# Decay sums spread over the partitions by two transfers through DRAM instead of PE transposes, gates formed between the chunks, in a two-layer hybrid trunk (one core)

## The reference, cut to what matters

```
proj = rms_norm(h) @ w_in
y_a  = gated DeltaNet(proj) @ w_out_gdn       # 8 heads, chunks
y_b  = sparse attention(proj) @ w_out_dsa     # 8 heads
h    = h + (sigmoid(g_a) * y_a + sigmoid(g_b) * y_b) @ w_o
h    = h + swiglu(rms_norm(h))
```

```
gam   = cumsum(g)                                        # per chunk
decay = exp(gam[:, None] - gam[None, :])  for i >= j     # chunk x chunk
q_dec, k_beta_dec = q * exp(gam), k * beta * exp(gam)
```

## Time and profile before

| | us |
|---|---|
| median of 3 runs (2181.29 to 2182.16) | 2181.73 |
| the profiled execution, its own time | 2180.09 |
| its span in the profile | 2178.3 |
| PE busy (share of the span) | 2146.1 (99%) |
| DVE, ACT, POOL busy | 1140.4, 1004.5, 1054.1 (52%, 46%, 48%) |
| mean granted clock of PE, as a share of full speed | 0.998 |
| DMA engines busy | 28.4% |

### The profile page before, as it was taken

One profiled execution on the slowest core, in us unless ns is written; L12 is line 12 of the kernel. 1 busy time (PEld: TensorE's weight loads), 2 busy tenths in 40 slices (PEclk: granted clock), 3 DMA queues, 4 the chain that ended last, 5 costly groups with the idle time before them and its releaser, 6 DMA issues.

```text
span 2178.3 us, 32534 instructions
## 1 busy us (share of the span) xinstructions
PE 2146.1 (99%) x12612; PEld 1764.5 (81%) x12612; DVE 1140.4 (52%) x2267; ACT 1004.5 (46%) x2285; POOL 1054.1 (48%) x776
## 2 busy tenths in 40 slices
PE   8999999999999999999999999999999999999998
PEld 6778887888888888888877788888888888888886
DVE  7678887444533444440187788765554234444302
ACT  6656665555423333332365656745554233333222
POOL 4455554433455555554445355534434555555542
PEclk9999999999999999999999999999999999999999
DMA  4222222222233333333322222222222333333332
GB/s 156 73 63 62 65 67 64 73 77 74 78 97 97 92 97 97 97 97 97 90 80 78 64 62 62 64 69 74 77 77 79 97 97 94 98 98 96 96 98 90
DMA packets 98937, 183.07 MB, mean 84 GB/s; under 512 B 11104, under 2 KB 11360, under 8 KB 98784
## 3 DMA queue, kind: packets, MB, share of 16 engines
q1 hardware_dynamic: 98784, 180.99, 28.4%
HBM read 178.85 MB, written 2.10 MB: 83 GB/s over the span
## 4 chain that ended last, share of the span: by engine, by line
PE 90%; DVE 5%; ACT 3%; POOL 1%; issue 1%; DMA 0%; DVEq 0%; SPq 0%; POOLq 0%; ACTq 0%
PE bank L1647 87%; PE bank L1723 2%; ACT w_hi L647 1%; DVE conv_acc L1082 1%; PE bank L2032 1%; DVE bank L1079 1%; DVE ob_lo L1079 1%; DVE inv L1079 1%; POOL w_lo L557 0%; ACT conv_acc L658 0%; PE bank L1717 0%; DVE left L1294 0%; ACT p_quad L658 0%; DVE k_b L1079 0%; POOL diagonal L588 0%
## 5 line engine op out<-in xcount | busy, mean ns | idle before, releaser
L557 POOL TENSOR_TENSOR w_lo<-w_raw,w_hi 128x512 fp32r<-128x512 f32 x668 | 927.8, 1411 | 1026.5 <-ACT w_hi L647 1026.5
L1647 PE MATMUL bank<-xn_hi,w_hi 128*128 128x512 f32 x1840 | 735.8, 400 | 3.0 <-POOL w_lo L557 2.0
L1647 PE MATMUL bank<-xn_hi,w_lo 128*128 128x512 f32 x1840 | 735.2, 400 | 0.0
L1647 PE MATMUL bank<-xn_lo,w_hi 128*128 128x512 f32 x1840 | 731.7, 398 | 0.0
L647 ACT ACTIVATE w_hi<-w_raw 128x512 fp32r<-128x512 f32 x668 | 385.2, 625 | 628.9 <-PE bank L1647 623.4
L1647 PEld LDWEIGHTS bank<-xn_hi,w_hi 128*128 128x128 f32 x1840 | 346.2, 188 | 76.6 <-issue 4.9
L1647 PEld LDWEIGHTS bank<-xn_hi,w_lo 128*128 128x128 f32 x1840 | 346.2, 188 | 70.7 <-issue 3.8
L1647 PEld LDWEIGHTS bank<-xn_lo,w_hi 128*128 128x128 f32 x1840 | 346.1, 188 | 68.4
L1079 DVE TENSOR_TENSOR residual<-residual,bank 128x512 f32<-128x512 f32 x32 | 22.0, 687 | 252.7 <-PE bank L1647 252.3
L1647 PE MATMUL bank<-mid_hi,w_hi 128*128 128x512 f32 x352 | 136.9, 389 | 0.0
L1647 PE MATMUL bank<-mid_lo,w_hi 128*128 128x512 f32 x352 | 136.9, 389 | 0.0
(11 more groups left out here) (274 smaller groups left out, 3207.9 us busy)
## 6 DMA issues: line engine op xcount, KB each, us to landing
w_raw<-w_tiles SPq DMA_DIRECT2D x668, 256.0 KB, 2.6
residual<-x_t SPq DMA_DIRECT2D x4, 512.0 KB, 6.1
out_t<-normalised SPq DMA_DIRECT2D x8, 256.0 KB, 2.2
rope<-rope SPq DMA_DIRECT2D x2, 512.0 KB, 6.0
mats<-mats SPq DMA_DIRECT2D x1, 320.0 KB, 3.1
vecs_all<-vecs SPq DMA_DIRECT2D x1, 129.0 KB, 7.5
mats<-mats SPq DMA_DIRECT2D x1, 128.0 KB, 7.0
vecs_all<-vecs SPq DMA_DIRECT2D x1, 4.0 KB, 1.7
```

The source lines that it names most:

```text
L557: nc.gpsimd.tensor_tensor(w_lo[j][:], w_raw[j][:], w_hi[j][:].bitcast(F32), ALU.subtract).then_inc(s_lo, 1)
L1647: return nc.tensor.matmul(out, lhsT, rhs, start=start, stop=stop)
```

## The change

Part by part:

1. **Rows by one more product.** Next to the two products that sum up g per chunk, PE makes a third, [32, 128], in which each partition is one chunk of one head. DVE copies it to `gam_rows`.
2. **Store and spread.** When tile 3 of the first front is done, SP waits for that copy and issues four stores of 8 rows x 128 numbers to a DRAM scratch in head order. One half tile later it waits until the stores have landed and issues the spread: one transfer that reads the pair's 1024 numbers for each of the 128 partitions, 512 KB, into `gam_b`. The spreads of pairs 1 to 3 are issued behind the second tile of their fronts.
3. **Gates from SBUF.** ACT forms Relu and Exp from `gam_b` in place of the PSUM banks: for pair 0 behind tile 3's tanh, for pairs 1 to 3 between the chunks of the pair before (head 0 after chunk 0, head 1 after chunk 1, both Exp after chunk 2). `q_d` is made from `gam_b` too. The copy of `hcol` moves from DVE to ACT.
4. **PE.** `head_gates` is gone, and so are its wait and two kinds of wait on `q_d` (stages qt and ot).
5. **Fill.** "mid" moves two dense products of each pair from T0 to P5; "last" moves four from T0 to O3, the stage before the outputs of pair 3.

```diff
-        head_p = steps("head_pe", two("kt", "gb"))
-        head_a = steps("head_act", two("sqk") + ["ga0", "sqrtk", "ga1"] + two("exp"))
+        head_p = steps("head_pe", two("kt"))
+        head_a = steps("head_act", ["hcol"] + two("ga") + two("exp") + two("sqk") + ["sqrtk"])
...
-        FILL_WEIGHT = {"mid": fill((12, 5, 4, 3, 3, 1, 34), (8, 9, 6, 3), (1, 2, 6), (7, 6, 5, 4), (6, 4, 6, 13)),
-                       "last": fill((9, 4, 4, 3, 2, 1, 33), (8, 9, 9, 3), (1, 2, 6), (5, 5, 4, 4), (5, 12, 8, 0))}
+        FILL_WEIGHT = {"mid": fill((12, 5, 4, 3, 3, 1, 32), (8, 9, 8, 3), (1, 2, 6), (7, 6, 5, 4), (6, 4, 6, 13)),
+                       "last": fill((9, 4, 4, 3, 2, 1, 29), (8, 9, 9, 3), (1, 2, 6), (5, 5, 4, 4), (5, 16, 8, 0))}
...
+            store_at = {ends_of(l, T0_GDN + 3): l for l in range(DEPTH)}
+            spread_at = {ends_of(l, T0_GDN + 8 * i + 1) if i else ends_of(l, T0_GDN + 3) + 1: (l, i)
+                         for l in range(DEPTH) for i in range(PAIRS)}
+
+            def store_rows(l):
+                sp.wait_ge(idx_v.sem, idx_v.after(l, "rows"))
+                by_chunk = gam_dram[l].rearrange("(h c t) -> c h t", h=NH, c=NC)
+                for c in range(NC):
+                    sp.dma_start(by_chunk[c], gam_rows[NH * c:NH * (c + 1), :]).then_inc(s_rows, 16)
+
+            def spread_rows(l, i):
+                sp.wait_ge(s_rows, 16 * NC * (l + 1))
+                if i:
+                    sp.wait_ge(gdn_a.sem, gdn_a.after(l * PAIRS + i - 1, "eg1"))
+                row = gam_dram[l, 2 * SEQ * i:2 * SEQ * (i + 1)]
+                sp.dma_start(gam_b[:].rearrange("p s t -> p (s t)"), row.partition_broadcast(P)).then_inc(s_gam, 16)
...
             def head_gate(l, i, s):
-                act.wait_ge(head_p.sem, head_p.after(t, f"gb{s}"))
+                act.wait_ge(s_gam, 16 * (t + 1))
+                act.wait_ge(head_a.sem, head_a.after(t, "hcol"))
...
+                    if i < PAIRS - 1:
+                        if c == 0:
+                            head_columns(l, i + 1)
+                            head_gate(l, i + 1, 0)
+                        if c == 1:
+                            head_gate(l, i + 1, 1)
+                        if c == 2:
+                            head_decays(l, i + 1)
                 if i < PAIRS - 1:
                     head_squares(l, i + 1)
-                    head_gate(l, i + 1, 0)
...
                     if m == 6:
-                        head_gate(l, 0, 0)
-                        head_rest(l, 0)
+                        head_root(l, 0)
...
+                    if m == 3:
+                        for j in range(2):
+                            head_gate(l, 0, j)
+                        head_decays(l, 0)
...
+                mm(bank[7][:NH * NC, P:2 * P], small[:, 14, :], mats[:, M_INCL, :])
...
-            def head_gates(l, i):
-                t = l * PAIRS + i
-                pe.wait_ge(head_v.sem, head_v.after(t, "hcol"))
-                for s in range(2):
-                    spread(by[s], hcol[:, s, 3, :]).then_inc(head_p.step(f"gb{s}"), 1)
```

More of the change, by code:

```diff
@@ L240, in hybrid_trunk @@
         d_tanh = sb("d_tanh", [SEQ], at=slot(53))
+        gam_rows = sb("gam_rows", [P], at=slot(53))
+        gam_b = sb("gam_b", [2, SEQ], at=slot(8))
+        gam_dram = nc.dram_tensor("gam_by_head", (DEPTH, NH * SEQ), F32, kind="Internal").ap()
         sg0 = slot(14)
@@ L742, in index @@
                 nc.scalar.activation(col_total[:], small[:, 10, :].rearrange(by_head, c=NC), ACT.Exp).then_inc(idx_a.step("etot"), 1)
+                act.wait_ge(idx_a.sem, idx_a.after(l, "ekd"))
+                head_columns(l, 0)
             def front(l, i, m, during, split_next=True):
@@ L784, in head_gate, with head_root, head_columns, head_decays @@
                 t = l * PAIRS + i
-                act.wait_ge(head_p.sem, head_p.after(t, f"gb{s}"))
+                act.wait_ge(s_gam, 16 * (t + 1))
+                act.wait_ge(head_a.sem, head_a.after(t, "hcol"))
                 for c in range(NC):
-                    last = nc.scalar.activation(decay[s][:, c, :], chunks(by[s])[:, c, :], ACT.Relu, bias=hcol[:, s, 3, c:c + 1], scale=-1.0)
+                    last = nc.scalar.activation(decay[s][:, c, :], gam_b[:, s, c * P:(c + 1) * P], ACT.Relu, bias=hcol[:, s, 3, c:c + 1], scale=-1.0)
                 last.then_inc(head_a.step(f"ga{s}"), 1)
-            def head_rest(l, i):
+            def head_root(l, i):
+                act.wait_ge(head_v.sem, head_v.after(l * PAIRS + i, "vark"))
+                nc.scalar.activation(rinv[:, :, 1, :], rinv[:, :, 1, :], ACT.Sqrt).then_inc(head_a.step("sqrtk"), 1)
+            def head_columns(l, i):
+                copy(hcol[:].rearrange("p s v c -> p s (v c)"),
+                     cols[:, 2 * i:2 * i + 2].rearrange("p h v c -> p h (v c)")).then_inc(head_a.step("hcol"), 1)
+            def head_decays(l, i):
                 t = l * PAIRS + i
-                act.wait_ge(head_v.sem, head_v.after(t, "vark"))
-                nc.scalar.activation(rinv[:, :, 1, :], rinv[:, :, 1, :], ACT.Sqrt).then_inc(head_a.step("sqrtk"), 1)
-                head_gate(l, i, 1)
                 for s in range(2):
@@ L820, in gdn @@
                 for s in range(2):
-                    nc.scalar.activation(q_d[s][:], chunks(by[s]), ACT.Exp).then_inc(gdn_a.step(f"eg{s}"), 1)
+                    nc.scalar.activation(q_d[s][:], gam_b[:, s, :].rearrange("p (c t) -> p c t", c=NC), ACT.Exp).then_inc(gdn_a.step(f"eg{s}"), 1)
                 if i > 0:
@@ L1229, in index @@
                 tt_(sm(11), sm(10), bank[7][:, :32], ALU.subtract).then_inc(idx_v.step("togo"), 1)
+                V.tensor_copy(gam_rows[:NH * NC, :], bank[7][:NH * NC, P:2 * P]).then_inc(idx_v.step("rows"), 1)
                 for what in ("t0_", "t1_", "t2_"):
@@ L1302, in head_columns @@
                 pair = slice(2 * i, 2 * i + 2)
-                V.tensor_copy(hcol[:].rearrange("p s v c -> p s (v c)"),
-                              cols[:, pair].rearrange("p h v c -> p h (v c)")).then_inc(head_v.step("hcol"), 1)
                 if i > 0:
@@ L1888, in gdn @@
                 for s in range(2):
-                    pe.wait_ge(gdn_a.sem, gdn_a.after(t, f"eg{s}"))
                     if i > 0:
```

19 lines of the change are left out of this document (11 added, 8 removed).

## The result

The changed kernel takes **2186.35 us** (median of 11 runs, 2184.18 to 2189.65), the kernel before 2181.31 in the same sessions: ratio 1.0025, 95% interval 1.0018 to 1.0033. It is slower by 5.0 us. The forecast was 2.9 us faster; it missed by 7.6 us, and the range, which ended at 2184.8, did not hold the result. The profiled run is the longest of the eleven, 2189.65 us with a span of 2187.8, 9.5 us over the span of before, so it shows more of each loss than the median does. The eleven runs' mean granted clocks lie at 0.995 to 0.997, and the time goes with them: 2186.3 to 2189.65 at 0.995, 2184.2 for both runs at 0.997. The profiled run of the kernel before has 0.998.

What follows compares the result with a forecast made beforehand. PE, busy in 99% of the span, was taken as the bound. Terms -7.1, +0.2, -2.4, +4.4, +1.2, +0.6 and +0.2 summed to -2.9 us: median 2178.8, own range 2175.5 to 2184, 8-in-10 range 2174.4 to 2184.8.

Steps and rivals of the forecast that it cites:

- terms 1 to 3: On PE: spreads leave, -7.1 us; one added product per layer, +0.2; POOL's wait in pair 0 goes, -2.4.
- step 4: Pair 0: ACT waits for the spread (3.8 us, landed at 82.5), so PE waits at tiles 6 and 7: +4.4 us.
- Step 5: Pairs 1 to 3: gates between the chunks fit ACT's idle gaps; cost 0.
- Step 7: Two dense products move into P5, where PE waits for ACT behind the same tile end; worth 0.
- part 4's second paragraph: Pair 0's spread: the skill's DMA figures estimate 3.2 us for it, which would make the sum 1.2 lower.
- step 6: Moved table load before DVE's chain, PE waiting at quads,below: +1.2 us in pairs 1 and 2, +0.6 pair 3, +0.2 pair 0.
- term 3: Pair 0, behind k_b: PE's 1.23 us wait for POOL's w_lo goes, -2.4 us in two layers.
- the late rival: Pair 0's spread lands late, at 86.4 with 7.7 us: sum +4.9, 2186.6 us; chance 0.12.
- step 1: PE's 64 hcol matmuls go: eight groups at 0.89 us each, -7.1 us, all on PE's path.
- the early one: Spread lands early, at 81.5, and the chain costs nothing: sum -6.9, 2174.8 us; chance 0.22.
- the table load with a further 1.4 us: ACT's table load costs some 1.4 us more, delaying the chain: sum +7.5, 2189.2 us; chance 0.03.

Runs made afterwards that it cites:

- fillback: Changed kernel with the dense products dealt as before the change (34 and 6 in pairs 0 to 2, 33 and 12 in pair 3): 2181.67 us.
- tab: Changed kernel plus one single-column Tanh on ACT right before the copies of kbT in each pair, bringing the table load forward: 2180.52 us.
- the padded kernel before: Kernel before the change with 194 idle PE instructions between early dense products, nothing else: 2183.24 us, ratio 1.0007.
- early: Changed kernel with the four stores one tile earlier and pair 0's spread half a tile after them: 2180.26 us, ratio to before 0.9999.
- best1 to best4: Changed kernel with earlier stores, old dense deal, later spreads: 2176.74 us; plus 125 idle PE instructions 2175.24; plus early table load instead 2172.65; plus both 2169.82.

## Why the prediction was wrong

Each term of the forecast's sum beside what the segments of PE's timeline say in the profiled run (two layers, us):

```
                                        forecast   measured
1  the spreads leave PE                   -7.1       -7.1
2  the added product                      +0.2       +0.2
3  POOL's wait in pair 0                  -2.4       -2.5
4  ACT waits for the spread, tiles 6, 7   +4.4       +5.2
6  pairs 1 and 2, chain                   +1.2       +1.2
6  pair 3, chain and what follows         +0.6       +1.2
6  pair 0, chain; 7, P5                   +0.2       +1.6
   stops and long SiLU in the small run    -         +3.6
   half clock                              -         +5.8
   this execution's late start             -         +0.7
   sum                                    -2.9       +9.9   (PE's end: +9.5)
```

**Right:** terms 1 to 3 within a tenth or two; the chain of step 4 with each link; the wait of 0.3 us in each of pairs 1 and 2; the 1.5 us in pair 3 (1.8 measured). Step 5, gates between the chunks at no cost, holds: PE has no new wait for `v_new`. Step 7 as it was put, that P5 waits as before behind the same tile end, is right: 0.25 to 0.37 us in three of the four pairs 1 and 2 with 8 products, against 0.36 with 6.

**Wrong, size:** the spread in step 4. The 3.8 us is the median of the eight, but that is luck, since the two that count took 4.6 and 4.7. They were issued 0.5 us earlier than forecast, and the term was 0.8 short. The 3.2 us of part 4's second paragraph lies under all eight, and the section that it comes from is on transfers that GpSimd issues, while these come from SP.

**Wrong, size:** pair 0 in step 6. I took 1.03 us of wait and added 0.1 per layer. PE had gained 1.24 per layer from term 3, and there that gain met the chain, which was 0.3 later from the start of the `kbT,k_f` products: before, POOL's `w_lo`, begun at 102.30, had held the diagonals until 107.70; now the table load held `a_t` until 108.73. The wait grew to 1.9 us while the two dense products that had covered it were issued at P5, where they cost their 0.45. That is 0.8 per layer, so a third of term 3 was given back; "fillback" and "tab" show both halves.

**Wrong, left out:** two things that no term held, so that the sum put them at nothing. They are where the prediction failed: together most of the distance from -2.9 to the result, and the stops alone outweigh the 2.9. The clock: the late rival had "a pause of PE that long could also lower the granted clock, for which no row has a price", but the forecast itself also had a pause of 2.0 us at tile 6, and gave it no clock. It took 5.8 us in the profiled run. In the median it is less: an estimate by the mean clocks, 0.996 in the median run against 0.998, gives some 4 (two rounded figures, so 2 to 6), and the median lies 2.1 above the two runs at 0.997. The stops: step 1 counted what 64 matmuls and their loads take, not that they are 148 instructions in a stream that comes in blocks. Stops and long SiLU took 3.6 us. Without the clock and the late start the measured terms sum to +3.4, and the two runs at 0.997 are 2.9 above the kernel before: so the change is slower even where the clock hardly fell, by the stops and by what steps 4 and 6 were short.

**The median and the range:** 2186.35 stands beside the late rival's 2186.6, by chance. The spread landed 0.3 us behind the forecast's time, not 3.9 us. The forecast's own range, too, doesn't come out of its two terms: landing at 81.7 to 84.2 and part 6 between 0 and 3 give 2175.2 to 2183.2, not 2175.5 to 2184. Of the other rivals, the early one and the table load with a further 1.4 us can be left: of 462 loads in the fourteen profiles 356 have their ACTIVATE within 1.31 us of the load's start, and the other 106 wait for data of DVE or PE.

## What to carry to other kernels

Price a pause of PE with its clock: of the 14 stretches at half clock in the profiles, the programs' ends left out, eleven begin 0.5 to 1.8 us behind a wait of 1.2 to 2.2 us (as the profile counts it), and the other three 2.2 to 2.4 us behind the 1.0 us at P5, with a wait of 1.8 some 12 us ahead. Many waits of that length have none behind them. Dealing two to four products back in front of such a wait, which I had priced at 1.3 us at most, was worth 4.7, about 1.2 of it at like clock. Before moving filler products away from a wait, look whether the wait's other side moves too; freeing PE ahead of a fixed chain only lengthens the wait. Where an ACT table switch must come, put one throw-away ACTIVATE into an idle stretch, and before shortening the PE program, expect runs of tiny products to meet a block edge elsewhere: 125 idle instructions were worth 0.7 to 2.8 us here.

## What the runs showed of the hardware that I had not expected

- PE stops for 0.25 to 1.7 us in runs of products that issue in 9 ns, where a 16 KB block of its code ends and the transfer on the instruction queue began less than some 2.4 us before PE got there; it goes on 2.2 to 2.9 us after that start. Moving the edge makes the stops come and go; what delays the transfer by up to a microsecond more in some pairs was not found. A spread in flight is not needed for it.
- An instruction of PE that only waits for a semaphore long up took 59 ns (90 of them moved the first product by 5.3 us), and nothing where it stood between dense products: from `mats,squares` to `mats,k_f` of layer 0, where all 194 of them lie in the padded kernel before, 67.35 us against 67.38 without them.
- A SiLU of DVE over 512 columns took 0.69 us alone and up to 2.4 beside POOL's `w_lo`; in pair 1 of layer 0 it ended 0.55 us after POOL's last one, however long it had taken.
- How many stretches at half clock follow the same waits varies from run to run: three in the profile of the changed kernel, none in that of "fillback", which still has waits of 1.4 to 1.8 us. The runs' times follow their mean clocks: "early" took 2178.4 to 2181.3 us in its eight runs at 0.997 and 2183.7 and 2183.8 in those at 0.995 and 0.994. Where the kernel has no wait over 1.4 us (before, best1 to best4), the mean is 0.996 to 0.998. No run changed the clock by itself, so its share is argued from these rows and not shown by an experiment.
